# Two model blocks on one core: two gate columns projected with the weights stationary, and a stage's first tile taken in two passes

## The chip, the cores and the metric

The program runs on 1 core of one Trainium2 chip. The metric is the device time of one execution in microseconds (us); lower is better. The time before is the median of 3 runs.

## The reference

The input is one sequence of 256 tokens with 1024 features, in float32. Two chains of layers are computed on it. The first is two layers of (a gated feed-forward block, a mixer, another feed-forward block), each around a residual and RMS norms. The mixer projects the normed tokens with one wide matrix and feeds a gated delta rule (GDN) and a convolution:

```python
p = h @ mix_w_in[i]
qkv, z, beta_logit, a_logit, glu_in, gates = jnp.split(p, SPLITS, axis=-1)
...
qkv = jax.nn.silu(causal_dwconv(qkv, conv_w))
beta = jax.nn.sigmoid(beta_logit.astype(jnp.float32))
g = -jnp.exp(a_log) * jax.nn.softplus(a_logit + dt_bias)
...
y = (g_a * y_a + g_b * y_b) @ mix_w_out[i]
x = x + rmsnorm(y, mix_norm_post[i])
```

`beta_logit` and `a_logit` are 8 columns each: together 16 columns of the 8208 of `mix_w_in`. They are called the gate columns here. The second chain has four layers, each a mixer (`gla`, `mla`, `conv`, `gla`), a squared-ReLU feed-forward block with 4096 hidden features (`mlp`), and a small gated block (`ple`):

```python
x = layer_norm(ALPHA * x + h, ln_g[i, 0], ln_b[i, 0])
x = layer_norm(ALPHA * x + jnp.square(jax.nn.relu(x @ mlp_w1[i])) @ mlp_w2[i], ln_g[i, 1], ln_b[i, 1])
x = x + jax.nn.sigmoid(x @ ple_w_gate[i]) * (p[i] @ ple_w_proj[i])
```

## The kernel before

**Tiles and precision.** The 256 tokens are two tiles of 128 (`NT` = 2, tile 0 and tile 1). The 1024 features are eight chunks of 128 (`KC` = 8). TensorE multiplies float32 as sums of three products: each operand is split into a high part (rounded, `..._hi`) and a low part (the rest, `..._lo`), and the kernel adds high x high, high x low and low x high. `h_hi`/`h_lo` are the two parts of the input of a stage, features on partitions and tokens along the free side.

**Weights.** All weights lie in one list of 128x1024 units. SyncE loads each unit into one of eight slots, ScalarE makes its high part (`weights`, L1459 to L1462) and VectorE its low part (L2007 to L2011); TensorE waits on the semaphore `w_lo` in `next_unit` and frees the slot through `w_used`. In the projections to q, k and v of the mixer only five slots are in use. The engines carry no scheduler: each engine's code is a list of stages (`STAGES`), and the order in which its instructions are written is the order in which they run; engines meet only at semaphores.

**How a stage begins.** The end of a stage leaves x (or its normed copy, or the mixer's y) with tokens on partitions. TensorE transposes a tile in two halves of four chunks (`begin_half` L656, `turn_half` L758), ScalarE copies each half out of PSUM as `h_hi` (L1490, L1493, L1499) and VectorE subtracts it from PSUM to get `h_lo` (L2044, L2048, L2055). TensorE then works on the first tile alone with the first four weight units: it waits for `h_lo` of tile 0, multiplies unit after unit, six matmuls of 512 columns for each, and before the fourth unit it transposes tile 1 (`begin_tile`). Then the same four units run on tile 1, where each unit is freed. This pattern stands in `ffn` (feed-forward stages, 8 of them: `ffn1`, `ffn2` of two layers and `mlp` of four), in `z` (the mixer's first stage, 2), in `project` for the stages whose tag ends in `.out` except the conv layer's (5: mix x2, gla x2, mla) and in `conv` (1). `gla`, `mla`, `gdn_out` and the `.g` branch of `project` have the same pattern in code of their own. In the `.out` stages of gla and mla the transposes of tile 0 come right before, with nothing between. `mlp` begins inside the last units of the product before it.

**The mixer's stages** run in the order z, glu, project16, qkv, mixer. `glu` makes eight chunks of the convolution's input. `project16` makes the gate columns: 48 matmuls, each with a 128x128 piece of `h` stationary and 16 columns of the weight unit moving, out 128 tokens x 16, a bank for each tile. VectorE copies them out (L2272) into `small`; a chain of short operations between VectorE (L2276 to L2285) and ScalarE (L1646 to L1654, with two table loads) follows, whose end (`decays`) is waited for by TensorE in `qkv` at chunk 8. `qkv` makes 24 chunks; for each, ScalarE takes the product out (L1624, L1627), VectorE does three taps of the short convolution (L2241) and a weight unit's low part, and ScalarE a Silu (L1634). Beside that VectorE has the 31 taps of the long convolution (`conv_taps`, L2319): a generator from which each `next` issues two operations. They are spread by hand over `glu`, `qkv` and `mixer`. `mixer` starts on TensorE with two weight units of the gates' products (`side`) and then waits for the last Silu of `qkv`.

## Time and profile before

| | us |
|---|---|
| median of 3 runs (lowest, highest) | 2905.0 (2901.14, 2905.58) |
| the profiled execution, its own time | 2903.36 |
| its span (first to last instruction) | 2901.5 |
| TensorE busy with matmuls | 2822.3 (97%) |
| VectorE busy, ScalarE busy | 1924.0, 1543.1 |

The mean granted clock of TensorE in that execution is 0.991 of full speed. A row of the timeline gives the start and the duration in us, the engine (PE = TensorE matmul, PEld = its weight loads, DVE = VectorE, ACT = ScalarE, POOL = GpSimd), the line of the kernel, the operation with out<-in and shapes, and in brackets the time for which the engine was idle before it, with what released it. Since matmuls overlap, the pace of TensorE is the distance from start to start, not the duration. Moving columns stand last in a matmul's shape: `128*16 128x256` is a stationary operand of 128 rows and 16 columns with 256 columns moving. Names in a matmul's row stand as out<-moving,stationary.

### The profile page before, as it was taken

To read this page: it belongs to the slowest core of one execution; us is meant where nothing else is said; L and a number is where in the kernel's file an instruction comes from. 1 tells how busy PE (TensorE), PEld (TensorE's weight loads), DVE (VectorE), ACT (ScalarE), POOL (GpSimd) and SP (SyncE) were. 2 spreads that over 40 slices of the span, in tenths; PEclk is the share of its full clock that TensorE was granted. 3 is DMA by queue.
4 is the path that set the end of the run, shared out by engine and by line. 5 is a ranking of instruction groups with operands and counts; after the bars stand their busy time and mean duration, and the time that the engine had idled before them with its cause. 6 is when DMAs were issued, how large, how long until landed. Compare 5 with 4: busy or idle time off the path is not lost.

```text
span 2901.5 us, 37886 instructions
## 1 busy us (share of the span) xinstructions
PE 2822.3 (97%) x15012; PEld 2386.3 (82%) x15012; DVE 1924.0 (66%) x2836; ACT 1543.1 (53%) x2389; POOL 71.8 (2%) x99
## 2 busy tenths in 40 slices
PE   8999999999999999999999999999999999999999
PEld 7879988788788799887888878887888888887887
DVE  5556998865565579888655864575546664577545
ACT  6544755565555547555555544454555454564544
POOL 0000000000000000000000000000000000000000
PEclk9999999999999999999999999999999999999999
DMA  8544420465465434115655345552654555542652
GB/s 299 187 139 165 162 73 23 174 208 188 151 218 187 169 122 153 52 42 205 210 188 184 131 157 188 174 187 96 214 188 168 185 198 186 183 161 94 207 184 78
DMA packets 127808, 470.00 MB, mean 162 GB/s; under 512 B 14494, under 2 KB 14654, under 8 KB 126480
## 3 DMA queue, kind: packets, MB, share of 16 engines
q1 hardware_dynamic: 124560, 453.08, 46.0%
q0 software_dynamic: 3072, 14.51, 1.4%
q8 instruction: 119, 1.95, 0.3%
q14 instruction: 57, 0.47, 0.1%
HBM read 466.48 MB, written 1.05 MB: 161 GB/s over the span
## 4 chain that ended last, share of the span: by engine, by line
PE 83%; DVE 11%; ACT 4%; issue 2%; POOL 0%; DMA 0%; POOLq 0%; DVEq 0%; SPq 0%; ACTq 0%
PE ps L619 79%; DVE w_lo_part L2011 2%; PE ps L785 2%; DVE conv_acc L2241 1%; DVE hc L2319 1%; ACT w_hi_part L1462 1%; PE ps L656 1%; DVE wx_lo_part L2011 1%; PE ps L1070 0%; DVE h_lo_part L2044 0%; ACT wx_hi_part L1462 0%; DVE x_res L2153 0%; DVE x_res L2211 0%; DVE x_res L2189 0%; POOL stats L2816 0%
## 5 line engine op out<-in xcount | busy, mean ns | idle before, releaser
L2011 DVE TENSOR_TENSOR w_lo_part<-w_raw,w_hi_part 128x1024 fp32r<-128x1024 f32 x459 | 552.5, 1216 | 317.0 <-ACT w_hi_part L1462 314.2
L1462 ACT ACTIVATE w_hi_part<-w_raw 128x1024 fp32r<-128x1024 f32 x459 | 478.6, 1057 | 355.0 <-PE ps L619 354.7
L619 PE MATMUL ps<-w_hi_part,h_hi_part 128*128 128x512 f32 (+1 forms) x1348 | 538.8, 400 | 24.7 <-DVE h_lo_part L2048 5.4
L619 PE MATMUL ps<-w_hi_part,h_lo_part 128*128 128x512 f32 (+1 forms) x1348 | 525.7, 390 | 0.0
L619 PE MATMUL ps<-w_lo_part,h_hi_part 128*128 128x512 f32 (+1 forms) x1348 | 525.2, 390 | 0.0
L2011 DVE TENSOR_TENSOR wx_lo_part<-wx_raw,wx_hi_part 128x1024 fp32r<-128x1024 f32 x222 | 268.3, 1220 | 193.5 <-ACT wx_hi_part L1462 191.8
L1462 ACT ACTIVATE wx_hi_part<-wx_raw 128x1024 fp32r<-128x1024 f32 x222 | 231.8, 1055 | 227.2 <-PE ps L619 226.9
L619 PEld LDWEIGHTS ps<-w_hi_part,h_hi_part 128*128 128x128 f32 x1348 | 255.9, 190 | 81.9 <-issue 12.5
L619 PEld LDWEIGHTS ps<-w_hi_part,h_lo_part 128*128 128x128 f32 x1348 | 256.1, 190 | 53.9
L619 PEld LDWEIGHTS ps<-w_lo_part,h_hi_part 128*128 128x128 f32 x1348 | 256.5, 190 | 47.8
L619 PE MATMUL ps<-wx_hi_part,h_hi_part 128*128 128x512 f32 x684 | 273.4, 400 | 7.1 <-ACT lv L1804 2.2
L619 PE MATMUL ps<-wx_lo_part,h_hi_part 128*128 128x512 f32 x684 | 268.2, 392 | 0.0
L619 PE MATMUL ps<-wx_hi_part,h_lo_part 128*128 128x512 f32 x684 | 268.2, 392 | 0.0
L619 PE MATMUL ps<-w_hi_part,hid_hi_part 128*128 128x512 f32 x528 | 206.1, 390 | 0.0
L619 PE MATMUL ps<-w_hi_part,hid_lo_part 128*128 128x512 f32 x528 | 205.5, 389 | 0.0
L619 PE MATMUL ps<-w_lo_part,hid_hi_part 128*128 128x512 f32 x528 | 205.4, 389 | 0.0
L2319 DVE SCALAR_TENSOR_TENSOR hc<-glu,cols,hc 128x256 f32<-128x256 f32 x480 | 198.5, 478 | 0.0
L619 PE MATMUL ps<-h_hi_part,w_hi_part 128*128 128x256 f32 (+1 forms) x680 | 195.5, 287 | 0.0
L619 PE MATMUL ps<-h_lo_part,w_hi_part 128*128 128x256 f32 (+1 forms) x680 | 194.5, 286 | 0.0
L619 PE MATMUL ps<-h_hi_part,w_lo_part 128*128 128x256 f32 (+1 forms) x680 | 194.4, 286 | 0.0
L619 PEld LDWEIGHTS ps<-wx_hi_part,h_hi_part 128*128 128x128 f32 x684 | 130.0, 190 | 36.1 <-issue 6.9
L2007 DVE SCALAR_TENSOR_TENSOR w_lo_part<-w_raw,cols,w_hi_part 128x512 fp32r<-128x512 f32 x110 | 82.6, 751 | 106.2 <-ACT w_hi_part L1460 106.2
(437 smaller groups left out, 4860.6 us busy)
## 6 DMA issues: line engine op xcount, KB each, us to landing
w_raw<-in_weights SPq DMA_DIRECT2D x569, 512.0 KB, 3.3
wx_raw<-in_weights SPq DMA_DIRECT2D x288, 512.0 KB, 3.3
row<-in_rows POOLq DMA_DIRECT2D x8, 1024.0 KB, 5.3
row<-in_rows POOLq DMA_DIRECT2D x8, 512.0 KB, 4.0
const<-in_const SPq DMA_DIRECT2D x1, 1088.0 KB, 8.5
x_res<-in_x SPq DMA_DIRECT2D x2, 512.0 KB, 5.3
ple_p<-in_p POOLq DMA_DIRECT2D x4, 256.0 KB, 5.1
out<-x_res SPq DMA_DIRECT2D x2, 512.0 KB, 2.6
```

Of the source, the lines that this page charges most:

```text
L619: return nc.tensor.matmul(out, lhsT, rhs_, start=start, stop=stop, skip_group_check=True)
L656: last_ = nc.tensor.transpose(turned_bank(t, b)[:, c, :], src[:, t, (4 * b + c) * P:(4 * b + c + 1) * P], ident)
L785: last_ = nc.tensor.transpose(hid_bank(c, blk // 2)[:, blk % 2, t * P:(t + 1) * P], hid[:, c % 2, t, blk * P:(blk + 1) * P], ident)
L1462: A(hi_of(s)[:, 0:wd], raw_of(s)[:, 0:wd], ACT.Copy).then_inc(*up("w_hi", u))
L2007: V.scalar_tensor_tensor(lo_of(s)[:, 0:BANK], raw_of(s)[:, 0:BANK], scale[0], hi[:, 0:BANK], ALU.mult, ALU.subtract)
L2011: V.tensor_tensor(lo_of(s)[:, 0:wd], raw_of(s)[:, 0:wd], hi[:, 0:wd], ALU.subtract).then_inc(*up("w_lo", u))
L2241: ins = V.scalar_tensor_tensor(cacc[:, c % 2, :], pre[:, c % 2, k:k + SEQ], col(("convw", i), c * CONV1 + k), cacc[:, c % 2, :], ALU.mult, ...
L2319: ins = V.scalar_tensor_tensor(hc[:, c, :], glu[:, c, k:k + SEQ], w, hc[:, c, :], ALU.mult, ALU.add)
```

## The change

The gate columns are computed turned: 16 weight columns stationary, 256 tokens moving, 24 matmuls into one bank, 16 partitions x 256. ScalarE copies the result to a free corner of `hc`, and after the first chunk of `qkv` TensorE transposes it back in two small transposes (`turn_small`) for VectorE. VectorE's weight unit and three steps of the long convolution, which stood ahead of the copy, now stand in the middle of the gate chain; ScalarE's weight unit stands behind its copy. TensorE's wait for `small` moves from chunk 2 to chunk 3.

The first tile of a stage is taken in two passes over its first four units in `ffn`, `z`, `conv` and the `.out` branch: first the 16 matmuls with `h_hi`, which wait only for `h_hi`; then the 8 with `h_lo`. Tile 1 is transposed after half of the second pass. Tile 1 is computed as before.

```diff
+            def row_high(s, out, hi, tok, start):
+                for n in range(2):
+                    c = slice(n * BANK, (n + 1) * BANK)
+                    mm(out(n), hi[:, tok], hi_of(s)[:, c], start, False)
+                    mm(out(n), hi[:, tok], lo_of(s)[:, c], False, False)
+            def row_low(s, out, lo, tok):
+                for n in range(2):
+                    mm(out(n), lo[:, tok], hi_of(s)[:, n * BANK:(n + 1) * BANK], False, False)
+            def first_tile(slots, out, what, between):
+                tok = slice(0, P)
+                pe.wait_ge(*when("h_hi", what))
+                for k in range(4):
+                    slots.append(next_unit())
+                    row_high(slots[k], out, h_hi[:, k, :], tok, k == 0)
+                pe.wait_ge(*when("h_lo", what))
+                for k in range(4):
+                    if k == 2:
+                        between()
+                    row_low(slots[k], out, h_lo[:, k, :], tok)
...
-                for t in range(NT):
-                    for j in range(4):
-                        if j % 2 == 0:
-                            pe.wait_ge(*when("h_lo", (tag, t, j // 2)))
-                        if t == 0:
-                            slots.append(next_unit())
-                        if t == 0 and j == 3:
-                            begin_tile(tag, 1)
-                        last_ = up_unit(slots[j], 0, j, t)
+                for j in range(4):
+                    if j % 2 == 0:
+                        pe.wait_ge(*when("h_hi", (tag, 0, j // 2)))
+                    slots.append(next_unit())
+                    up_unit(slots[j], 0, j, 0, low=False)
+                for j in range(4):
+                    if j == 2:
+                        begin_tile(tag, 1)
+                    if j % 2 == 0:
+                        pe.wait_ge(*when("h_lo", (tag, 0, j // 2)))
+                    up_unit(slots[j], 0, j, 0, high=False)
...
             def project16(tag):
                 pe.wait_ge(*when("evacuated", (tag + ".z", 1)))
                 s = next_unit()
+                out = ps[0:16, 2, 0:SEQ]
+                for k in range(KC):
+                    c = slice(k * 16, (k + 1) * 16)
+                    mm(out, hi_of(s)[:, c], h_hi[:, k, :], k == 0, False)
+                    mm(out, hi_of(s)[:, c], h_lo[:, k, :], False, False)
+                    last_ = mm(out, lo_of(s)[:, c], h_hi[:, k, :], False, k == KC - 1)
+                last_.then_inc(*up("w_used", ("small", tag)))
+            def turn_small(tag):
+                pe.wait_ge(*when("small_out", tag))
                 for t in range(NT):
-                    for k in range(KC):
...
+                    last_ = nc.tensor.transpose(ps[:, 3, t * 16:(t + 1) * 16], hc[0:16, KC - 1, t * P:(t + 1) * P], ident[0:16, 0:16])
+                last_.then_inc(*up("turned", ("small", tag)))
...
             def project16(tag):
+                act.wait_ge(*when("w_used", ("small", tag)))
+                A(hc[0:16, KC - 1, :], ps[0:16, 2, 0:SEQ], ACT.Copy).then_inc(*up("small_out", tag))
                 weights(1)
```

TensorE at the start of the first gla layer's `.out` stage, before; behind these rows come the other three units, six matmuls each, with the transposes of tile 1 (L758) ahead of the fourth:

```order
L758 MATMUL ps<-const,xn 128x128 [waits y]
L758 MATMUL ps<-const,xn 128x128 x3
L619 MATMUL ps<-w_hi_part,h_hi_part 128x512 [waits w_lo,h_lo]
L619 MATMUL ps<-w_lo_part,h_hi_part 128x512
L619 MATMUL ps<-w_hi_part,h_lo_part 128x512
```

The same place, the change (`turn_half` is L781 there); the first three rows open the pass over four units, and the rows with `h_lo_part` are the second pass around the transposes of tile 1:

```order
L619 MATMUL ps<-w_hi_part,h_hi_part 128x512 [waits w_lo,h_hi]
L619 MATMUL ps<-w_lo_part,h_hi_part 128x512
L619 MATMUL ps<-w_hi_part,h_hi_part 128x512
...
L619 MATMUL ps<-w_hi_part,h_lo_part 128x512 [waits h_lo]
L619 MATMUL ps<-w_hi_part,h_lo_part 128x512 x3
L781 MATMUL ps<-const,xn 128x128 [waits y]
L781 MATMUL ps<-const,xn 128x128 x3
...
L619 MATMUL ps<-w_hi_part,h_lo_part 128x512 x4
```

The first wait is now for `h_hi` alone. The transposes of tile 1 stand after 20 matmuls instead of 18, and 4 matmuls of tile 0 are left behind them instead of 6.

VectorE from the last chunk of `glu` to the start of `qkv` in the first layer, before:

```order
L2011 TENSOR_TENSOR w_lo_part<-w_raw,w_hi_part 128x1024 [waits w_hi] x2
L2319 SCALAR_TENSOR_TENSOR hc<-glu,cols,hc 128x256 [waits conv] x8
L2011 TENSOR_TENSOR w_lo_part<-w_raw,w_hi_part 128x1024 [waits w_hi]
L2272 COPY small<-ps 128x32 [waits w_used]
...
L2281 TENSOR_SCALAR small<-small 128x2x8 [waits a_in]
L2283 TENSOR_TENSOR small<-small 128x2x8 [waits softplus,v_step]
```

The same place, the change (the line numbers of the kernel after):

```order
L2052 TENSOR_TENSOR w_lo_part<-w_raw,w_hi_part 128x1024 [waits w_hi] x2
L2362 SCALAR_TENSOR_TENSOR hc<-glu,cols,hc 128x256 [waits conv] x2
L2312 COPY small<-ps 128x32 [waits turned]
...
L2321 TENSOR_SCALAR small<-small 128x2x8 [waits a_in]
L2052 TENSOR_TENSOR w_lo_part<-w_raw,w_hi_part 128x1024 [waits w_hi,v_step]
L2362 SCALAR_TENSOR_TENSOR hc<-glu,cols,hc 128x256 [waits conv] x6
L2326 TENSOR_TENSOR small<-small 128x2x8 [waits softplus]
```

Six of the eight tap operations and the weight unit's low part moved from ahead of the copy to the place where VectorE waits for ScalarE's softplus; the work is the same.

## Rows read from the trace of the kernel before

**Rows 1.** The page, part 1: TensorE's busy time, share and instructions.
```profile
PE 2822.3 (97%) x15012; PEld 2386.3 (82%) x15012; DVE 1924.0 (66%) x2836; ACT 1543.1 (53%) x2389; POOL 71.8 (2%) x99
```

**Rows 2.** Who TensorE waited for: total us, times, longest (VectorE at L2355, in `gdn_out`).
```profile
PE ps L619 <- DVE gdn_w L2355: 7.0, 2, 3.5
```

**Rows 3.** Stretches: length; busy (instructions) of PE, PEld, DVE, ACT, POOL; clock; DMA.
```profile
279.30:285.20 5.90, 5.90 (x50) 5.90 (x48) 4.76 (x9) 2.36 (x3) 0.00 (x0) 0.88 0.33 103
285.30:290.50 5.20, 5.20 (x25) 5.20 (x26) 3.24 (x9) 3.51 (x7) 0.00 (x0) 0.50 0.53 179
1579.90:1582.70 2.80, 2.80 (x25) 2.23 (x24) 2.80 (x3) 1.06 (x1) 0.00 (x0) 1.00 0.93 315
```

**Rows 4.** Timeline of VectorE from the end of `glu` into `qkv`.
```profile
283.20 3.25 DVE L2319 SCALAR_TENSOR_TENSOR hc<-glu,cols,hc 128x256 f32<-128x256 f32 x8
286.61 1.22 DVE L2011 TENSOR_TENSOR w_lo_part<-w_raw,w_hi_part 128x1024 fp32r<-128x1024 f32 x1 [0.16 <-ACT w_hi_part L1462]
287.75 0.18 DVE L2272 COPY small<-ps 128x32 f32<-128x32 f32 x1
...
291.69 0.17 DVE L2283 TENSOR_TENSOR small<-small 128x16 f32<-128x16 f32 x1 [2.85 <-ACT small L1654]
...
292.33 1.53 DVE L2241 SCALAR_TENSOR_TENSOR conv_acc<-conv_pre,cols,conv_acc 128x256 f32<-128x256 f32 x3 [0.25 <-ACT conv_acc L1627]
...
319.23 1.53 DVE L2241 SCALAR_TENSOR_TENSOR conv_acc<-conv_pre,cols,conv_acc 128x256 f32<-128x256 f32 x3 [0.47 <-ACT conv_acc L1627]
...
362.72 1.52 DVE L2241 SCALAR_TENSOR_TENSOR conv_acc<-conv_pre,cols,conv_acc 128x256 f32<-128x256 f32 x3
```

**Rows 5.** Timeline of TensorE where `mixer` begins.
```profile
363.81 0.39 PE L619 MATMUL ps<-w_hi_part,h_lo_part 128*128 128x512 f32 x1
364.75 1.16 PE L619 MATMUL ps<-const,gdn_gate 128*128 128x128 f32 x8 [0.55 <-ACT qkvT L1634]
```

**Rows 6.** Stretches behind three idle times of TensorE, columns as in rows 3.
```profile
1319.50:1324.70 5.20, 5.20 (x16) 4.51 (x17) 5.20 (x6) 1.37 (x2) 0.57 (x1) 0.50 0.63 187
1679.80:1683.10 3.30, 3.30 (x9) 2.55 (x8) 1.07 (x3) 0.00 (x0) 0.00 (x0) 0.50 0.00 0
...
2657.50:2661.00 3.50, 3.49 (x15) 2.91 (x16) 2.15 (x5) 0.00 (x0) 0.46 (x1) 1.00 0.02 5
```

**Rows 7.** Timeline, first tile of the first gla layer's `.out` stage: ScalarE, VectorE, TensorE.
```profile
1676.32 0.60 ACT L1499 ACTIVATE h_hi_part<-ps 128x512 fp32r<-128x512 f32 x1 [2.52 <-PE ps L758]
...
1677.99 1.28 DVE L2055 TENSOR_TENSOR h_lo_part<-ps,h_hi_part 128x512 fp32r<-128x512 f32 x2
...
1678.73 0.50 PE L619 MATMUL ps<-w_hi_part,h_hi_part 128*128 128x512 f32 x1 [1.67 <-DVE h_lo_part L2055]
```

**Rows 8.** The same stage, tile 1: transposes, `h_lo`, its first matmul.
```profile
1684.55 1.03 PE L758 MATMUL ps<-const,xn 128*128 128x128 f32 x8
...
1685.82 1.29 DVE L2055 TENSOR_TENSOR h_lo_part<-ps,h_hi_part 128x512 fp32r<-128x512 f32 x2 [4.94 <-ACT h_hi_part L1499]
...
1686.80 0.39 PE L619 MATMUL ps<-w_hi_part,h_hi_part 128*128 128x512 f32 x1
```

**Rows 9.** Timeline, start of `z` in the first layer: ScalarE and TensorE.
```profile
204.80 2.17 ACT L1493 ACTIVATE h_hi_part<-ps,cols 128x128 fp32r<-128x128 f32 x8 [1.74 <-PE ps L656]
...
207.33 0.79 PE L619 MATMUL ps<-w_hi_part,h_hi_part 128*128 128x512 f32 x1 [2.13 <-DVE h_lo_part L2048]
```

**Rows 10.** Timeline of TensorE, first matmul of mla's `.out` stage.
```profile
1992.50 0.50 PE L619 MATMUL ps<-w_hi_part,h_hi_part 128*128 128x512 f32 x1 [0.97 <-DVE h_lo_part L2055]
```

**Rows 11.** Timeline, first `mlp` stage: TensorE's third unit, VectorE's x, tile 1's first matmul.
```profile
1707.59 0.50 PE L619 MATMUL ps<-wx_hi_part,h_hi_part 128*128 128x512 f32 x1 [0.23 <-DVE h_lo_part L2044]
...
1708.27 1.41 DVE L2211 SCALAR_TENSOR_TENSOR x_res<-xn,stats,row 128x512 f32<-128x512 f32 x2 [0.67 <-POOL stats L2816]
...
1711.62 0.39 PE L619 MATMUL ps<-w_hi_part,h_hi_part 128*128 128x512 f32 x1
```

**Rows 12.** Timeline, `ffn2` of the first layer: tile 1's first matmul.
```profile
608.52 0.50 PE L619 MATMUL ps<-w_hi_part,h_hi_part 128*128 128x512 f32 x1 [1.57 <-DVE h_lo_part L2044]
```

More of the change, by code:

```diff
@@ L731, in project, with turn_second @@
                         turn_half(ready, 0, 1)
[L732 to L742 removed]
+                    def turn_second():
+                        turn_half(ready, 1, 0)
+                        turn_half(ready, 1, 1)
+                    first_tile(slots, lambda n: out(0, n), (ready, 0, 0), turn_second)
+                    pe.wait_ge(*when("h_lo", (ready, 1, 0)))
+                    for k in range(4):
+                        row_chunk(slots[k], out, h_hi[:, k, :], h_lo[:, k, :], 0, k == 0, False, tiles=[1]).then_inc(*up("w_used"))
                     for t in range(NT):
@@ L894, in z @@
                 slots = []
-                for t in range(NT):
-                    pe.wait_ge(*when("h_lo", (tag, t, 0)))
-                    for k in range(4):
-                        if t == 0:
-                            slots.append(next_unit())
-                        if t == 0 and k == 3:
-                            begin_tile(tag, 1)
-                        last_ = row_chunk(slots[k], out, h_hi[:, k, :], h_lo[:, k, :], 0, k == 0, False, tiles=[t])
-                        if t == 1:
-                            last_.then_inc(*up("w_used"))
+                first_tile(slots, lambda n: out(0, n), (tag, 0, 0), lambda: begin_tile(tag, 1))
+                pe.wait_ge(*when("h_lo", (tag, 1, 0)))
+                for k in range(4):
+                    row_chunk(slots[k], out, h_hi[:, k, :], h_lo[:, k, :], 0, k == 0, False, tiles=[1]).then_inc(*up("w_used"))
                 for t in range(NT):
@@ L1355, in conv, with up_unit @@
             def conv(tag, j):
-                def up_unit(s, c, j, t):
+                def up_unit(s, c, j, t, high=True, low=True):
                     tok = slice(t * P, (t + 1) * P)
@@ L2269, in project16 @@
             def project16(tag):
-                weights(1)
-                dve.wait_ge(*when("w_used", ("small", tag)))
-                V.tensor_copy(small[:, 0:2, :], ps[:, 2:4, 0:16]).then_inc(*up("small", tag))
+                dve.wait_ge(*when("turned", ("small", tag)))
+                V.tensor_copy(small[:, 0:2, :], ps[:, 3, 0:32].rearrange("p (t n) -> p t n", t=NT)).then_inc(*up("small", tag))
                 dve.wait_ge(*when("small", tag))
@@ L2281, in project16 @@
                 link(V.tensor_scalar(small[:, 12:14, 0:GH], small[:, 2:4, 0:GH], 0.0, None, ALU.max))
+                weights(1)
+                for _ in range(3):
+                    next(taps[0])
                 dve.wait_ge(*when("softplus", tag))
@@ L2297, in glu_ @@
                     if c >= 4:
-                        for _ in range(4):
+                        for _ in range(4 if c < KC - 1 else 1):
                             next(taps[0])
```

77 lines of the change are left out of this document (37 added, 40 removed).

## The prediction

> **What bounds the kernel now.** I read the page first: TensorE is busy 97% of the span [rows 1], so only two things can be saved: work of TensorE itself, and the short waits between stages. The list of who TensorE waited for shows that these are single waits of 0.2 to 3.5 us [rows 2, 7]. Then I read the places the change touches in the timeline. The reader should look at starts, since TensorE's pace is start to start.
>
> **Gate columns, on TensorE.** The 48 narrow matmuls fill 279.3 to 285.3, 6.0 us [rows 3]. They go at the pace of their weight loads, not of their 16 columns: the stretch has 48 loads in 5.9 us. And they bring the clock down: it is 0.88 of full in that stretch and 0.50 (1.2 GHz) in the 5.2 us behind it, where 25 matmuls of `qkv` take 5.2 us. The turned form exists already in gla: its 24 matmuls take 2.8 us at clock 1.00 [rows 3]. At full clock the 25 matmuls of `qkv` would take 25 x 0.12 = 3.0 us (0.12 is 2.8/24 rounded up). So TensorE saves 6.0 - 2.8 = 3.2 us and 2.2 us of slow clock, and pays some 0.2 us for two small transposes: 5.2 us in each of the two mixers.
>
> Here a rule speaks against the change. The rows show 48 matmuls of 16 columns at 0.12 us each [rows 3]. The Trainium skill (TensorE: Matmul & The Clock Gate, "Wait — 56ns, not 53.3ns?") says that back-to-back matmuls start as little as about 25 ns apart when they are narrow; by that floor alone 48 would be an estimated 1.2 us, and turning them into 24 of 256 columns would lose time. The measured pace is five times that floor, so the rows decide. None of the sum rests on this page.
>
> **Gate columns, on the path.** What TensorE saves isn't what the kernel saves. The mixer's first matmul waits for the last Silu of `qkv`, and is already 0.55 us late [rows 5]: VectorE works through `qkv` almost without a pause from 292.33 to 362.72, 23 chunks in 70.4 us, 3.06 us each, where TensorE needs 24 x 0.12 = 2.9 us [rows 4]. So `mixer` starts when VectorE is done, and the question is how much earlier VectorE starts `qkv`. Before: eight tap operations 283.20 to 286.45, the weight unit to 287.8, copy at 287.75, short chain, 2.85 us idle for softplus, then `qkv` at 292.33. After: two tap operations end at about 284.0. The copy waits for TensorE: turned products 279.3 to 282.1, first chunk of `qkv` 2.9 us to 285.0, transposes and their latency 0.4 us, copy at 285.4. The short operations take 1.1 us (287.75 to 288.84, where the idle time of 2.85 us begins), to 286.5; the weight unit 1.1, to 287.6; six tap operations 6 x 0.41 = 2.45 (3.25/8), to 290.05. Softplus comes 3.8 us after the copy's end (287.93 to 291.69; ScalarE has two table loads in it), so at 285.6 + 3.8 = 289.4, and is hidden. `qkv` then starts 0.6 us behind, as before (291.69 to 292.33): 290.6, 1.7 us earlier. The pause of 0.47 us at 319.23 [rows 4] came from TensorE's late chunk and goes. So each mixer starts 2.2 us earlier, not 5.2. The three other us become idle time of TensorE ahead of `mixer`: 0.55 + 5.2 - 2.2 = about 3.5 us.
>
> **A price that the trace of before doesn't show at this place.** TensorE's idle times of 3.5 us elsewhere [rows 2] have the clock at 0.50 behind them for 5.2 us of work (the first of [rows 6]). Below, nothing is lost if the clock holds, as it did behind an idle time of 1.7 us in the second gla layer (1.00) while it fell behind the same one in the first (0.50) [rows 6]. Above, 5.2 us at half speed lose 2.6 us, if all of it is on the path. The start of `mixer` is mostly TensorE bursts, with ScalarE and VectorE beside them; I take 2.0 us, nearer the upper end, since the idle time is like the 3.5 us one. The gate part is then worth 2 x (2.2 - 2.0) = 0.4 us, of which both ends are 2 x 2.2 = 4.4 and 2 x (-0.4) = -0.8.
>
> **Waiting for `h_hi` only.** Gain by stage, from the first matmul's new start:
> - gla `.out`, twice: `h_hi` ends at 1676.92, so the first matmul can start at about 1677.0; it now starts at 1678.73, because VectorE begins `h_lo` only at 1677.99 [rows 7]. Gain 1.7 us each. The second pass needs `h_lo` after 16 matmuls, 3.6 us, when it is long there. In the first of them the clock fell to 0.50 for 3.3 us [rows 6]; with 1.7 us less idle I expect it to hold, another 1.65 us (half of 3.3), once.
> - mla `.out`: idle 0.97 us [rows 10], of which `h_lo`'s first half, about 0.7 us, goes.
> - `z`, twice: eight copies in 2.17 us from 204.80, so half 0 is there at 205.9, against 207.33 now [rows 9]. But 1.3 us earlier at slow clock is three matmuls, 0.7 us at full clock, and the next point takes 0.45 of it: 0.3 us each.
> - `mlp`, four times: before, the third unit waits for `h_lo` of half 1 (a gap of 0.23 us, and as much for restarting) [rows 11]; the first pass fills it. Gain 0.45 us each, about as much as tile 1 can take: VectorE gives its x from 1708.27 on, so TensorE's transposes can't move, and tile 1's first matmul comes at 1711.15 instead of 1711.62.
> - `ffn2` twice and `ffn1` of layer 1: tile 1 is 1.57 us late for VectorE's reasons [rows 12]: nothing.
> - `mix` `.out` twice, `conv`, first stage: no wait for `h_lo` there, or one for weights: nothing.
>
> **What the new order costs.** Tile 1's transposes come after 20 matmuls instead of 18, with 4 behind them instead of 6. Before: transposes at 1684.55, `h_lo` of half 0 at 1686.47, first matmul at 1686.80, 0.33 us later [rows 8]. Now two matmuls of cover, 0.45 us, are gone: TensorE waits 0.15 to 0.2 us. That takes 0.2 from each of the gla and mla gains and makes the four stages without a gain 0.2 us longer each. It is inside the figures given for `z` and `mlp`.
>
> Sum of the first tiles: 2 x 1.5 + 0.5 + 2 x 0.3 + 4 x 0.45 - 4 x 0.2 = 5.1, and 1.65 of clock: 6.75 us. With the gates' 0.4: 7.15 us. Against the profiled execution's own 2903.36 us (1.6 below the median of 2905.0) that is **2896.2 us**, said as 2896.
>
> **The rivals.**
> 1. The clock holds at the mixer's start, and comes back sooner at `z`. For it: stretches behind similar idle times fell and held [rows 6]. Against: the longest idle times fell. Gain 4.4 + 6.75 + up to 2 x 1.7 (half of 3.4) = 11 to 14.5, say 2891. The 1.7 is half of a stretch like the 3.3 us one [rows 6].
> 2. TensorE's saving goes through whole, because VectorE has slack in `qkv` that I don't see: 2 x 5.2 + 6.75 = 17, 2886. Against: VectorE's pace of 3.06 us a chunk [rows 4] and the wait at 364.75 [rows 5].
> 3. Tile 1 eats the gains: VectorE's and ScalarE's order is unchanged, so an earlier TensorE waits for the next thing of theirs (y, x, `h_lo` of tile 1), and no clock is won. Half of 5.1 and -0.8 for the gates, 2901.5. For it: `ffn2`'s wait of 1.57 us [rows 12]. Against: in gla, TensorE reaches tile 1's transposes at 1677.0 + 20 x 0.23 = 1681.6, and y of tile 1 is VectorE's next work behind the `h_lo` that ends at 1679.27 [rows 7], 2.3 us before.
> 4. Slower: the first pass asks for four weight units in 2.7 us (12 matmuls) instead of 4.1 us (18). If a stage's third and fourth units were split only behind the stage's start, each would cost ScalarE and VectorE 1.1 to 1.2 us, some 2.3 us in 15 stages: 34 us, 2930. It decides if VectorE has a weight unit between the last product and the first tile's units. Against: the first gla tile ran 18 matmuls behind its start with no wait for `w_lo`, and VectorE has none between rows 7 and rows 8.
>
> **How the numbers follow.** My forecast gets 0.55, rival 1 0.20, rival 2 0.04, rival 3 0.19, rival 4 0.02. The range takes the forecast with its bounds (4.4 to -0.8 for the gates, clock won or not), rival 1 to 2889 and rival 3 to 2902; outside are rivals 2, 4 and some of the scatter of 4 us that the runs before have among themselves: **2889 to 2902**. A measurement of this kernel tells about 0.2% from no change, 5.8 us: faster means under 2899.2. That is most of the forecast (0.50 of 0.55), rivals 1 and 2 and nothing of rival 3: 0.74. Same 0.24, slower 0.02.
>
> **What the profile after would show.** Right: 24 matmuls of shape 128*16 128x256 in 2.8 us at clock 1.00 and no 0.50 stretch behind them; VectorE without the 2.85 us idle, with one of about 1.4 us ahead of its copy; TensorE idle about 3.5 us at the start of `mixer`, probably with 0.50 behind it; the first matmul of gla `.out` 0.1 us behind `h_hi`; 0.1 to 0.3 us waits at tile 1. Wrong: a mixer start that moves by 5 us, waits of TensorE on `w_lo` in first tiles, or a clock that falls at the turned form after all.

## The result, and the profile after

The kernel before took 2905.0 us (median of 5 runs, 2901.14 to 2905.58), the changed one 2889.43 (2885.91 to 2890.74): ratio 0.9949, with a 95% interval of 0.9938 to 0.996. The profiled execution of the changed kernel took 2885.91 us with a span of 2884.0, which is 17.5 less than the span before. Its mean granted clock is 0.996; before it was 0.991. So the time fell by 15.6 us where 9 were forecast: the sign is right, the time lies at the low end of the range, and most of this text is on where the other 7 us come from.

The page, part 1:

```profile
PE 2808.7 (97%) x14968; PEld 2371.0 (82%) x14968; DVE 1923.6 (67%) x2836; ACT 1542.2 (53%) x2391; POOL 71.9 (2%) x99
```

TensorE's busy time fell by 13.6 us [rows 1], with only 44 matmuls fewer. Two pieces of that are the gate columns. Stretches of the changed kernel (columns as in rows 3): the turned products, the work behind them, and the start of the mixer.

```profile
278.40:281.20 2.80, 2.80 (x27) 2.33 (x27) 1.56 (x2) 2.37 (x3) 0.00 (x0) 1.00 0.00 0
281.30:286.50 5.20, 5.20 (x44) 5.04 (x43) 3.81 (x10) 3.08 (x6) 0.00 (x0) 1.00 0.62 202
360.10:365.30 5.20, 5.20 (x39) 4.94 (x40) 4.85 (x14) 4.43 (x19) 0.82 (x1) 1.00 0.69 249
```

The products take 2.8 us instead of 6.0, and the clock is 1.00 behind them where it was 0.50: 44 matmuls in 5.2 us instead of 25 [rows 3]. That much was forecast. The third row was not: the clock holds at the mixer's start too.

VectorE around the gate columns, and its first chunk of `qkv`; the last row is its last chunk:

```profile
282.40 0.87 DVE L2362 SCALAR_TENSOR_TENSOR hc<-glu,cols,hc 128x256 f32<-128x256 f32 x2
284.49 0.19 DVE L2312 COPY small<-ps 128x32 f32<-128x32 f32 x1 [1.22 <-PE ps L953]
...
285.62 1.22 DVE L2052 TENSOR_TENSOR w_lo_part<-w_raw,w_hi_part 128x1024 fp32r<-128x1024 f32 x1
286.76 2.46 DVE L2362 SCALAR_TENSOR_TENSOR hc<-glu,cols,hc 128x256 f32<-128x256 f32 x6
289.14 0.17 DVE L2326 TENSOR_TENSOR small<-small 128x16 f32<-128x16 f32 x1
...
289.57 1.52 DVE L2282 SCALAR_TENSOR_TENSOR conv_acc<-conv_pre,cols,conv_acc 128x256 f32<-128x256 f32 x3
```

The idle time of 2.85 us ahead of softplus [rows 4] is gone, and one of 1.22 stands ahead of the copy: both as forecast. But between 289.57 and the mixer's start VectorE has no idle time over 0.2 us any more. Before there were two, of 0.47 us at 319.23 [rows 4] and of 1.41 us at 327.01, and the forecast counted only the first. The second one, before:

```profile
327.01 1.53 DVE L2241 SCALAR_TENSOR_TENSOR conv_acc<-conv_pre,cols,conv_acc 128x256 f32<-128x256 f32 x3 [1.41 <-ACT conv_acc L1627]
```

TensorE at the mixer's start, after:

```profile
357.74 0.39 PE L619 MATMUL ps<-w_hi_part,h_lo_part 128*128 128x512 f32 x1
360.10 1.16 PE L619 MATMUL ps<-const,gdn_gate 128*128 128x128 f32 x8 [1.97 <-ACT qkvT L1673]
```

It waits 1.97 us there, not 3.5, and the mixer starts 4.65 us earlier than before [rows 5]. Tile 1 of `z` already starts 0.80 us earlier than before (215.94 against 216.74), so 3.85 belong to the gates' part, where the forecast had 2.2.

The first tiles. The three lines are the start of `z`, of the first gla `.out` stage and of mla's `.out`:

```profile
206.86 0.80 PE L619 MATMUL ps<-w_hi_part,h_hi_part 128*128 128x512 f32 x1 [0.80 <-ACT h_hi_part L1532]
...
1667.14 0.50 PE L619 MATMUL ps<-w_hi_part,h_hi_part 128*128 128x512 f32 x1
...
1977.10 0.50 PE L619 MATMUL ps<-w_hi_part,h_hi_part 128*128 128x512 f32 x1 [0.25 <-ACT h_hi_part L1538]
```

`h_lo` no longer holds any of the three. `z` waits 0.80 us for ScalarE's `h_hi` instead of 2.13 for `h_lo` [rows 9], mla 0.25 instead of 0.97 [rows 10], and gla's matmul starts without idle time, where it had waited 1.67 [rows 7]; it stands 0.05 us behind the end of `h_hi`:

```profile
1666.49 0.60 ACT L1538 ACTIVATE h_hi_part<-ps 128x512 fp32r<-128x512 f32 x1 [2.51 <-PE ps L781]
```

In the gla stage the first matmul stands 1.34 us behind the first transpose (1665.80) instead of 3.11 (1675.62): 1.77 us, forecast 1.7. The price, tile 1 of gla and of `z`:

```profile
1671.83 1.03 PE L781 MATMUL ps<-const,xn 128*128 128x128 f32 x8
1672.62 1.17 PE L619 MATMUL ps<-wx_hi_part,h_lo_part 128*128 128x512 f32 x4
1673.84 0.50 PE L619 MATMUL ps<-w_hi_part,h_hi_part 128*128 128x512 f32 x1
```

```profile
215.94 0.50 PE L619 MATMUL ps<-w_hi_part,h_hi_part 128*128 128x512 f32 x1 [1.04 <-DVE h_lo_part L2089]
```

In gla the four matmuls behind the transposes need 0.92 us at full pace and the next one comes 1.22 after them: 0.3 us of waiting, forecast 0.15 to 0.2. In `z` the distance from start to start is 1.43 us, where it was 0.97: 0.46, the whole of the two matmuls of cover.

**The clock.** A list of all stretches at 0.50 in the two profiles shows what else changed. Before, behind the start of the program and ahead of its last matmul: 6.83 us long at 205.3, 283.8, 983.5, 1062.0, 1318.0 and 2304.5, 3.41 at 543.2, 1679.8 and 1939.2. After: 3.41 at 206.5, 537.5 and 977.9, 6.83 at 1309.0 and 2288.6. Half of TensorE's busy time in them is 22.4 us before and 10.6 us after. So up to 11.8 of the 17.5 us are clock. Two of the stretches (283.8 and 1062.0) went with the narrow matmuls; whether the others went for a reason or by chance one profile can't say.

### The profile page after: what moved, and what is told of

Its sections match the earlier page's. It is cut to its first block, busy times and chain, and to the rows that moved or that the text cites. A ratio compares the mean times of both kernels' runs of the same rounds, so it can differ in the third digit from the quotient of the medians.

```text
span 2884.0 us, 37784 instructions
## 1 busy us (share of the span) xinstructions
PE 2808.7 (97%) x14968; PEld 2371.0 (82%) x14968; DVE 1923.6 (67%) x2836; ACT 1542.2 (53%) x2391; POOL 71.9 (2%) x99
## 4 chain that ended last, share of the span: by engine, by line
PE 81%; DVE 13%; ACT 4%; issue 2%; POOL 0%; DMA 0%; POOLq 0%; SPq 0%; DVEq 0%; ACTq 0%
PE ps L619 77%; DVE w_lo_part L2052 3%; DVE conv_acc L2282 2%; PE ps L810 2%; DVE hc L2362 2%; PE ps L681 1%; ACT w_hi_part L1501 1%; DVE wx_lo_part L2052 1%; PE ps L1102 0%; ACT wx_hi_part L1501 0%; DVE h_lo_part L2085 0%; DVE x_res L2252 0%; POOL stats L2859 0%; DVE gdn_w L2398 0%; DVE x_res L2194 0%
## 5 line engine op out<-in xcount | busy, mean ns | idle before, releaser
L619 PE MATMUL ps<-w_hi_part,h_hi_part 128*128 128x512 f32 x1316 | 530.6, 403 | 20.0 <-DVE h_lo_part L2085 4.6
L619 PE MATMUL ps<-w_lo_part,h_hi_part 128*128 128x512 f32 x1316 | 516.2, 392 | 0.0
L619 PE MATMUL ps<-w_hi_part,h_lo_part 128*128 128x512 f32 x1316 | 505.2, 392 | 0.0
L619 PEld LDWEIGHTS ps<-w_hi_part,h_hi_part 128*128 128x128 f32 x1316 | 249.5, 190 | 79.8 <-issue 12.9
L619 PEld LDWEIGHTS ps<-w_hi_part,h_lo_part 128*128 128x128 f32 x1316 | 246.7, 188 | 52.3
L619 PEld LDWEIGHTS ps<-w_lo_part,h_hi_part 128*128 128x128 f32 x1316 | 249.9, 190 | 47.7
```

Source lines behind the costliest of these rows:

```text
L619: return nc.tensor.matmul(out, lhsT, rhs_, start=start, stop=stop, skip_group_check=True)
```

## The experiments

### The two parts, and the two halves of the gates' part

Four kernels, on one chip, each with 11 runs beside 33 of the kernel before (median 2903.24). `e1_gates` is the kernel before with every edit on the gate columns; `e2_passes` with every edit on first tiles; `e3_form` has the turned product, but VectorE's order as before:

```diff
             def project16(tag):
                 weights(1)
-                dve.wait_ge(*when("w_used", ("small", tag)))
-                V.tensor_copy(small[:, 0:2, :], ps[:, 2:4, 0:16]).then_inc(*up("small", tag))
+                dve.wait_ge(*when("turned", ("small", tag)))
+                V.tensor_copy(small[:, 0:2, :], ps[:, 3, 0:32].rearrange("p (t n) -> p t n", t=NT)).then_inc(*up("small", tag))
```

(TensorE's and ScalarE's side of the form is as in the change), and `e4_order` keeps the 48 narrow matmuls, with VectorE's new order around its old copy; the three steps of the long convolution are taken from the last chunk of `glu`:

```diff
             def project16(tag):
-                weights(1)
                 dve.wait_ge(*when("w_used", ("small", tag)))
...
+                weights(1)
+                for _ in range(3):
+                    next(taps[0])
                 dve.wait_ge(*when("softplus", tag))
```

**e1_gates.** 

> The gate columns' part alone (turned products, moved VectorE work, transposes back); first tiles as before. Theory A (VectorE's chain through qkv sets the mixer's start, and its start of qkv and its two pauses moved): each mixer starts 3.85 us earlier than before against the stage z (start of mixer minus start of tile 1 in z: 144.2 us instead of 148.0), TensorE idle about 2 us there, clock not at 0.50 behind it; 2 x 3.85 = 7.7 us, time near 2897. Theory B (the two parts only work together, the gates' part alone gives what the prediction said, 0.4 us): mixer 2.2 us earlier and a slow stretch behind it, 2904. Theory C (TensorE's 5.2 us per mixer go through): 2894.

**e2_passes.** 

> The two passes of first tiles alone; gate columns as before. Theory A (parts are additive; the trace of the whole change puts 17.5 us of span against before, 7.7 of them at the gates and 1.5 at a slow stretch that wanders): 8 us, 2897, of which z gives 1.7 to 2.3 us each, the gla .out stages 1.8 to 2.9 each, mla .out 0.4, mlp 0.3 to 0.5 each, and the first stage, conv and mix .out lose 0.2 to 1 us each. Rival (z's gain comes from the gates' part or is a matter of chance in the clock; the prediction's 0.3 each stands): z 0.3 each, sum 5 us, 2900.

**e3_form.** 

> The turned form alone: 24 matmuls with 256 columns, transposed back, but VectorE's weight unit and eight tap operations ahead of its copy as before. Theory A (VectorE sets the mixer's start): VectorE starts qkv at about the same time as before (292.3), so only the pauses of 0.47 and 1.41 us inside qkv can go: mixer 0.5 to 1.9 us earlier each, 1 to 4 us in all, 2901 to 2904; TensorE idle 3.9 to 5.2 us ahead of the mixer, and by the prediction's reading of the clock a 0.50 stretch behind it, which takes up to 2 us back. Theory C (TensorE's saving counts): mixer 5 us earlier, 2894.5.

**e4_order.** 

> VectorE's moved order alone: weight unit and six tap operations inside the gate chain; 48 narrow matmuls as before. Theory A: VectorE starts qkv 1.7 to 2 us earlier than 292.3, but TensorE is late by its own work (the 6.0 us and the slow clock remain), so the mixer can start only 0.55 us earlier, the idle time there: 0 to 1 us in all, 2904 to 2905. If TensorE lags, VectorE's pause in qkv grows instead. Rival (the order alone brings the 3.85 us): 2897.

Measured: e1_gates 2897.51 us (ratio 0.998, 0.9971 to 0.9989), e2_passes 2899.61 (0.9987, 0.9978 to 0.9996), e3_form 2900.25 (0.999, 0.9981 to 0.9998), e4_order 2901.42 (0.9997, 0.9988 to 1.0006, so no gain is shown for it).

In e1_gates the mixer starts 144.17 us behind tile 1 of `z`, where it was 148.01 before, and 3.84 earlier in the second layer too. That is theory A (3.85), and not B (2.2) or C (5.2). By the medians the kernel is 5.7 us faster than the one before, where theory A had 7.7; the clock, below, is where A was wrong. The halves show how it is made up. VectorE's two pauses inside `qkv` in e4_order, where the narrow matmuls stayed:

```profile
319.76 1.53 DVE L2241 SCALAR_TENSOR_TENSOR conv_acc<-conv_pre,cols,conv_acc 128x256 f32<-128x256 f32 x3 [0.99 <-ACT conv_acc L1627]
...
327.54 1.52 DVE L2241 SCALAR_TENSOR_TENSOR conv_acc<-conv_pre,cols,conv_acc 128x256 f32<-128x256 f32 x3 [1.42 <-ACT conv_acc L1627]
```

and in e3_form, with the turned product but the old order:

```profile
293.24 0.17 DVE L2293 TENSOR_TENSOR small<-small 128x16 f32<-128x16 f32 x1 [2.85 <-ACT small L1664]
...
323.92 1.52 DVE L2251 SCALAR_TENSOR_TENSOR conv_acc<-conv_pre,cols,conv_acc 128x256 f32<-128x256 f32 x3
...
326.71 1.52 DVE L2251 SCALAR_TENSOR_TENSOR conv_acc<-conv_pre,cols,conv_acc 128x256 f32<-128x256 f32 x3
```

So the form alone removes both pauses (0.47 + 1.41 = 1.88 us) and leaves the 2.85 us idle; the order alone removes the 2.85 and leaves, even lengthens, the pauses. Behind tile 1 of `z` the mixer of e4_order starts 1.5 us earlier than before in the first layer, where the slow stretch behind the narrow matmuls was 3.41 us long, and 0.1 later in the second, where it was 6.83: TensorE's lateness takes back what VectorE's order wins. Together they give the 3.85: VectorE begins `qkv` at 289.57 instead of 292.33, 1.96 us earlier beside the 0.80 from before, and 1.88 are the pauses. Why the second pause goes, ScalarE shows. Before, from chunk 9 (counted from 0) to the Silu ahead of chunk 11:

```profile
318.45 0.39 ACT L1624 ACTIVATE conv_pre<-ps 128x256 f32<-128x256 f32 x1 [2.66 <-PE ps L619]
...
323.05 1.28 ACT L1631 ACT_TABLE_LOAD   x1
324.34 0.27 ACT L1631 ACTIVATE gdn_gate<-gdn_gate 128x80 f32<-128x80 f32 x1
324.63 1.28 ACT L1634 ACT_TABLE_LOAD   x1
325.92 0.42 ACT L1634 ACTIVATE qkvT<-conv_acc 128x256 f32<-128x256 f32 x1
```

and the changed kernel:

```profile
316.98 1.28 ACT L1670 ACT_TABLE_LOAD   x1
319.71 0.27 ACT L1670 ACTIVATE gdn_gate<-gdn_gate 128x80 f32<-128x80 f32 x1 [1.46 <-DVE gdn_gate L2295]
320.00 1.28 ACT L1673 ACT_TABLE_LOAD   x1
```

The Exp of the decays needs a table of its own, one load ahead of it and one behind. Before, ScalarE had waited 2.66 us for TensorE's late chunk, so it came to the Exp late, and both loads (2.9 us with the Exp) stood ahead of the next chunk for VectorE. Now TensorE is ahead, ScalarE is through with its chunk sooner, and the first load runs while ScalarE would wait for VectorE anyway (the 1.46 us ahead of the Exp). In e3_form the Exp waits in the same way, for 1.54 us, and in e4_order both loads stand ahead of the next chunk as before: the pause goes with the form. That the table loads are its middle link is read from these rows; no run removed them alone. (The Trainium skill, ScalarE: Activation LUTs, "What ACT_TABLE_LOAD costs", gives 1283 ns for the load and 1380 ns of draining, 2.66 us for a switch. The trace agrees with the 1.28; the drain isn't seen, since the Exp begins 1.29 us behind the load's start.)

e3_form speaks against C as well: TensorE's whole saving is there, but the mixer starts only 2.1 us earlier (against tile 1 of `z`), and the other 3.2 are wait, 4.11 us from start to start instead of 0.94:

```profile
364.44 1.86 PE L619 MATMUL ps<-const,gdn_gate 128*128 128x128 f32 x7 [3.72 <-ACT qkvT L1642]
```

The clock is another matter. In e1_gates it fell at the mixer's start in both layers, behind the same wait of 2.37 us at which it had held in the changed kernel. The first layer's stretch:

```profile
362.90:368.10 5.20, 5.20 (x33) 5.20 (x33) 4.38 (x13) 3.98 (x18) 0.36 (x1) 0.67 0.65 240
```

And the slow stretch at 1679.8, which the prediction wanted to remove by a shorter idle time, is in none of e1_gates, e3_form and e4_order, though their gla `.out` stage waits for `h_lo` as before. So it was a matter of the one profile, not of the idle time alone. In e2_passes the first matmul of `z` comes 1.88 us behind the first transpose instead of 3.23, yet little of that is left at the mixer: `z` to `mixer` takes 160.21 and 160.42 us instead of 160.65 and 160.79, and both `z` have their 6.83 us slow as before. The prediction's 0.3 for `z` is met there, and e2_passes' own theory A (1.7 to 2.3) is not; its median, 3.6 us under the kernel before, is nearer the 5 of its rival than the 8 of A. The gla and mla stages gain in it what they gain in the whole change: the first matmul of gla `.out` comes 1.34 us behind the first transpose in both gla layers.

### Is it chance? The changed kernel again, and z undone

`e5_again` and `e11_third` are the changed kernel unedited, with the next kernels on their chips; `e8_zold` is the changed kernel with the old first tile in `z` alone; `e6_t18` transposes tile 1 two matmuls sooner:

```diff
                 for k in range(4):
-                    if k == 2:
+                    if k == 1:
                         between()
                     row_low(slots[k], out, h_lo[:, k, :], tok)
...
-                    if j == 2:
+                    if j == 1:
                         begin_tile(tag, 1)
```

and `e7_taps` moves three steps of the long convolution:

```diff
-                    if c % 2:
+                    if c % 2 and c > 3:
                         next(taps[0])
...
-                        for _ in range(4 if c < KC - 1 else 1):
+                        for _ in range((4, 4, 6, 2)[c - 4]):
                             next(taps[0])
```

**e5_again.** 

> The changed kernel itself once more, unedited. The two parts alone gave 5.7 and 3.6 us by their medians, 9.4 together, where the whole change gave 15.6 in another comparison; its records had a mean clock of 0.994 to 0.996, those of the parts 0.990 to 0.994. Theory D (the parts work together: only in the whole change does the clock hold at the mixer's start and come back sooner in z): median near 2888, clock 0.994 or more in nearly all runs, slow stretches behind the mixer's start in none. Rival E (which idle time is followed by slow clock is largely chance, and the profiled run was a lucky one): median 2890 to 2894, clocks from 0.991 to 0.996, and the profile shows a slow stretch at places where the first had none.

**e6_t18.** 

> The changed kernel with the transposes of tile 1 after 18 matmuls again (the first half of the second pass is two matmuls, six stand behind the transposes), in all four places. Theory (the wait at tile 1 is the two matmuls of cover): in z the wait from start to start falls from 1.43 to 0.97 us, the waits at tile 1 of mla's and gla's .out go, each of the 15 stages gains 0 to 0.46 us where VectorE's x is not what it waits for: 1.5 to 4 us in all against the changed kernel, 2886. Rival (x or y of tile 1 comes too late for an earlier transpose, the wait only moves ahead of the transposes): same as the changed kernel within 1 us.

**e7_taps.** 

> The changed kernel with three steps of the long convolution (two operations each, 0.81 us a step) moved by hand into VectorE's idle times in glu (2.10 us ahead of chunk 7, 1.22 ahead of the copy): two of them out of the first chunks of qkv, one out of the end of the mixer. Theory A (VectorE sets the mixer's start): mixer starts 2 x 0.81 = 1.6 us earlier, the wait there falls from 2.36 to 0.8 us from start to start, and the wait for the last tap before the mixer's end shrinks by up to 0.8: 2 x (1.6 + 0.8) = 4.8 us at most, 2885. Rival (something else, ScalarE's Silus or TensorE, sets the start): less than 1 us each.

**e8_zold.** 

> The changed kernel with z's first tile in the old order. By the profiles of the whole change z gave 1.67 and 2.29 us. Theory (the whole of it is z's earlier start of 1.3 us at the first matmul plus a slow stretch of 3.41 instead of 6.83 us, less 0.46 at tile 1): this kernel is 3 to 4 us slower than the changed one, and has 6.83 us slow in both z. Rival (what the clock gave was chance; the shift of the first matmul is nearly given back): 0.6 to 1.7 us slower.

Measured, 5 runs each beside a kernel before of 2902.86 us: e5_again 2890.55 (0.9956, 0.9942 to 0.9969), e6_t18 2888.52 (0.9952, 0.994 to 0.9965), e7_taps 2885.27 (0.9942, 0.9929 to 0.9954), e8_zold 2892.99 (0.9966, 0.9954 to 0.9979).

The change is there again with its two repeats (0.9949, 0.9956, 0.9947 with e11_third below). e5_again goes to rival E. Its profile has slow clock where the first had none, at the second layer's mixer (stretch of e5_again):

```profile
1135.74:1140.94 5.20, 5.20 (x32) 5.20 (x33) 3.64 (x9) 3.20 (x18) 0.00 (x0) 0.67 0.69 212
207.50:214.20 6.70, 6.00 (x14) 4.75 (x15) 3.83 (x12) 2.71 (x9) 2.37 (x4) 0.50 0.25 79
```

and its first `z` is slow for 6.83 us, the second row, while e11_third, the same program, has the same place like this:

```profile
207.50:214.20 6.70, 6.33 (x23) 5.11 (x24) 3.50 (x11) 2.38 (x8) 2.37 (x4) 0.75 0.29 83
```

23 matmuls against 14 in the same 6.7 us. So the place of the slow clock is in part chance, but not chance alone. From the first transpose of `z` to the mixer's start, in us, with the slow time in `z`:

| | layer 1 | layer 2 |
|---|---|---|
| before | 160.65 (6.83) | 160.79 (6.83) |
| e2_passes | 160.21 (6.83) | 160.42 (6.83) |
| e1_gates | 156.51 (6.83) | 156.71 (6.83) |
| e8_zold | 156.48 (6.83) | 156.48 (6.83) |
| changed kernel | 155.13 (3.41) | 154.65 (3.41) |
| e5_again | 156.56 (6.83) | 155.29 (3.41) |
| e11_third | 155.14 (3.41) | 154.70 (3.41) |

With the old first tile, `z` had 6.83 us slow in all 10 cases of five kernels (the one before, e1_gates, e3_form, e4_order, e8_zold, two layers each). With the new one it had 3.41 in 9 of 16 (eight profiles). Where it stays 6.83 the new order gives 0 to 0.4 us, and where it is 3.41 it gives 1.2 to 2.0. So the earlier start doesn't only pull matmuls into slow time: with it full clock often comes back sooner. The profiles show that the two go together, not why. e8_zold's median is 2.4 us above e5_again's, between its theory (3 to 4) and its rival (0.6 to 1.7), with overlapping intervals.

At the mixer's start with a wait of about 2.4 us the clock fell in 6 of 12 cases (e1_gates 2, e8_zold 2, e5_again 1, e6_t18 1; the changed kernel and e11_third none), and the mixer's first part grew by 0.5 us in e1_gates' first layer, by 1.2 in e5_again's second. The six are not spread evenly: with the old first tile in `z` (e1_gates, e8_zold) it fell in 4 of 4, with the new one in 2 of 8. The order of first tiles in `z` may thus bear on the clock at the mixer as well, 155 us later; 12 cases can't settle it.

e6_t18: the wait at tile 1 of `z` is 0.97 from start to start again, as expected:

```profile
214.61 0.50 PE L619 MATMUL ps<-w_hi_part,h_hi_part 128*128 128x512 f32 x1 [0.57 <-DVE h_lo_part L2089]
```

Its median is 2.0 us better than e5_again's, at the low end of what was expected, and the intervals overlap. Of that 1.55 us are seen in the traces: 0.46 in each `z`, and 0.21 in each of gla (twice) and mla, where the wait at tile 1 is gone (gla from the first transpose to tile 1's first matmul 7.83 us instead of 8.04). The rest is not told apart from the clock.

e7_taps confirms theory A where its work went as planned. First layer:

```profile
358.47 0.39 PE L619 MATMUL ps<-w_hi_part,h_lo_part 128*128 128x512 f32 x1
359.39 1.16 PE L619 MATMUL ps<-const,gdn_gate 128*128 128x128 f32 x8 [0.53 <-ACT qkvT L1673]
```

The wait fell from 2.36 to 0.92 from start to start, and that for the last tap of the convolution from 1.98 to 1.17. In the second layer the wait only fell to 1.94: there `glu`'s idle times of VectorE are 2.20 and 2.11 us ahead of chunks 5 and 6 and none ahead of 7, so steps put behind chunk 6 only made it later. The kernel is 5.3 us better than e5_again by the medians, where at most 4.8 were expected; 3.5 of them are seen in the traces (1.45 and 0.41 at the two mixers, 0.8 at the last tap of each), and the rest is not told apart from the clock.

### The price of the clock at 3.6 us of idle time, and the best version

`e10_idle` brings about the idle time that the prediction had expected at the mixer:

```diff
-                    if c % 2:
+                    for _ in range(2 if c in (5, 7) else c % 2):
                         next(taps[0])
```

`e9_best` is e6_t18 with e7_taps' edit, its numbers by layer:

```diff
-                        for _ in range(4 if c < KC - 1 else 1):
+                        for _ in range(((4, 4, 6, 2), (5, 5, 4, 2))[i][c - 4]):
```

**e10_idle.** 

> The changed kernel with two more steps of the long convolution (2 x 0.81 us of VectorE) in the middle of qkv, taken from its end in the mixer: TensorE's wait ahead of the mixer becomes 2.36 + 1.63 = 4.0 us from start to start, 3.6 idle, which is the idle time of the prediction. The prediction's price: slow clock behind it in both layers, 2.0 us each. Theory now (five slow stretches of 3.41 us behind waits of 2.4 us cost 0.5 to 1.2 us each from the mixer's start to its last tap, 1.3 and 1.8 behind waits of 4.1 us): slow in both layers, 1.3 to 1.8 us each. Apart from the clock, the mixer starts 1.63 later and the last tap is 1.63 earlier in VectorE's chain, so most of that comes back at the wait for the last tap (1.98 before): sum 3 to 5 us slower than the changed kernel by either, or 1 to 2 if the clock costs nothing there.

**e9_best.** 

> Both improvements together: the transposes of tile 1 after 18 matmuls, and three steps of the long convolution earlier, this time by a table for each layer (4, 4, 6, 2 steps behind chunks 4 to 7 of glu in the first layer, 5, 5, 4, 2 in the second, since there VectorE's idle time lies ahead of chunks 5 and 6). Theory A: as the two alone (2.0 and 5.3 us against the changed kernel by their medians), 6 to 7.5 us, and the second layer's mixer wait falls from 2.37 to about 0.9 us as the first one's did (it was 1.94 with one table for both): 2882 to 2885. Rival (the two share their gain, since a stage can only be as early as VectorE): 2885 or more.

**e11_third.** 

> The changed kernel once more, unedited, as the measure for the two beside it and for a third profile of its clock: by theory E (chance) 2888 to 2892, with slow stretches behind z's start of 3.41 us in about half the cases and 6.83 in the others, and behind the mixer's start in about half.

Measured, 5 runs each, the kernel before 2904.78 us beside them: e10_idle 2891.14 (0.9956, 0.9943 to 0.9968), e9_best 2884.5 (0.9935, 0.9921 to 0.9949), e11_third 2887.96 (0.9947, 0.9934 to 0.9959).

TensorE at the first mixer of e10_idle, and the stretches behind the start in both layers:

```profile
363.97 1.44 PE L619 MATMUL ps<-const,gdn_gate 128*128 128x128 f32 x5 [3.61 <-ACT qkvT L1673]
```

```profile
363.97:369.20 5.23, 5.23 (x24) 5.23 (x25) 3.60 (x8) 3.14 (x18) 0.00 (x0) 0.50 0.70 245
1139.00:1144.20 5.20, 5.20 (x24) 5.20 (x25) 3.59 (x8) 3.11 (x18) 0.00 (x0) 0.50 0.66 236
```

24 matmuls in 5.2 us, where the changed kernel had 39 [its row above]. The next matmul that waits for VectorE (operand `gdn_w`) comes 29.60 us behind the mixer's start instead of 27.88: the slow clock costs 1.72 us, and 1.64 in the second layer. The two rows are of e10_idle and of the changed kernel:

```profile
393.57 0.68 PE L619 MATMUL ps<-gdn_w 128*128 128x128 f32 x4 [0.37 <-DVE gdn_w L2479]
```

```profile
387.98 0.79 PE L619 MATMUL ps<-gdn_w 128*128 128x128 f32 x5 [0.60 <-DVE gdn_w L2479]
```

e3_form, with a wait of 4.11 us, has 29.66 there, and 29.19 in the second layer, where the slow stretch was 3.41 us long instead of 6.83. The prediction's price of 2.0 us at 3.5 us of idle time was about right; the idle time was not. The kernel is 3.2 us slower than e11_third, as expected.

e9_best has the short wait in both layers. The second one's:

```profile
1129.36 0.39 PE L619 MATMUL ps<-w_hi_part,h_lo_part 128*128 128x512 f32 x1
1130.31 1.16 PE L619 MATMUL ps<-const,gdn_gate 128*128 128x128 f32 x8 [0.56 <-ACT qkvT L1673]
```

It takes 154.68 and 154.70 us from `z` to the mixer with 6.83 us slow in both, 1.9 less than e5_again's 156.56 in the same case. It is the fastest kernel tried by its median, 20.3 us under the kernel before and 3.5 under e11_third; its interval and e11_third's overlap, so that it beats the changed kernel is likely, not shown by the times alone. Its time lies in the range of its theory A (2882 to 2885) and its second layer's wait fell as expected, but against the changed kernel beside it the gain is 3.5 us, where theory A added up 6 to 7.5: the two gains had been taken against e5_again, where the changed kernel had gained least of its three comparisons. Against e7_taps (2885.27, on another chip) it can't be ranked.

## Why the prediction was right or wrong

**What bounds the kernel.** Right: TensorE stays busy 97%, and everything won is waits between stages, work of TensorE and clock.

**Gate columns on TensorE.** Right in each number: 2.8 us at clock 1.00, the slow stretch behind it gone in both layers and in every kernel with the form, gone in none without it (before, e2_passes, e4_order).

**Gate columns on the path.** The method was right: VectorE sets the mixer's start, not TensorE's 5.2 us. The term was mis-sized at one sentence: "The pause of 0.47 us at 319.23 came from TensorE's late chunk and goes. So each mixer starts 2.2 us earlier". The rows of VectorE through `qkv` hold one more pause, 1.41 us at 327.01, ended by ScalarE; it isn't in the text. It came from TensorE's lateness in the second degree, by way of the table loads, and goes too (e3_form against e4_order). With VectorE's start 1.96 earlier instead of 1.7, the term is 3.85 instead of 2.2.

**The clock's price at the mixer.** The price of 2.0 was near the 1.72 measured by e10_idle, but was put on 3.5 us of idle time. (Of the two idle times of 3.5 us that it was modelled on, one had slow clock for 6.83 us behind it, at 1318.0, the other for 3.41, at 543.2; the text shows only the first.) With 1.65 us more of VectorE's chain gone, 1.97 are left, and behind that the clock falls in half of the cases for 0.5 to 1.2 us. So the gates' term is 2 x 3.85 less some 2 x 0.4, about 7, not 0.4. By medians e1_gates is 5.7 us under the kernel before. The two together, the pause that wasn't counted and the price put on an idle time that shrank with it, carry most of the miss.

**`h_hi` only.** gla `.out` with tile 1: 1675.62 to 1686.80 before, 1665.80 to 1673.84 after, 3.14 us less, of which 1.65 are the slow stretch; 1.49 remain, forecast 1.5. The second gla layer, at full clock in both profiles, has 9.59 (2654.40 to 2663.99) and 8.05 (2638.60 to 2646.65): 1.54. `mlp`: from tile 0's transposes to tile 1's first matmul 9.48 before (1702.14 to 1711.62), 9.01 after (1689.31 to 1698.32): 0.47, forecast 0.45. mla with its `mlp` 0.74, forecast 0.95; conv with its `mlp` 0.4 (2180.39 to 2495.17 before, 2164.97 to 2479.34 after), forecast 0.25: 0.4 are lost at `conv`'s own first tile and 0.8 won behind it. That can't be told from the scatter: e2_passes has -0.1 there, and e11_third, with the slow stretch of `conv` 3.41 us long instead of 6.83, 1.1. `ffn2` and tile 1's transposes there: nothing won, and `mix` `.out` longer by 0.2, as forecast. `z`: 0.3 was the value for slow clock of 6.83 us; it missed that the earlier start halves it in 9 of 16 cases, so that the mean is nearer 1. The 1.65 us of clock at gla stand in the profile before and in none of the three other profiles with the old order there, so the reason given (a shorter idle time lets the clock hold) is not what made them go.

**Order of tile 1.** Right: 0.3 us in gla, 0.46 in `z`, undone by e6_t18.

**The rivals.** The first (the clock holds, comes back sooner at `z`; 2891) came nearest to the time, and its two events happen, each about half of the time; but of the missing 7 us only about half are the clock's price at the mixer; as much is VectorE's earlier end (2 x 1.65), which it doesn't have. The second was right that there was slack in `qkv` which the text didn't see, and wrong on its size: e3_form shows TensorE's saving stopped by VectorE. Of the third only the waits at tile 1 are seen, 0.3 to 0.46 us. The fourth did not occur at its size of 34 us. In the profile after, no first tile waits for `w_lo`, except the program's first matmul, as before; but in three of the other profiles with the new order (e5_again, e10_idle, e11_third) the program's very first tile has one more such wait, 0.3 to 0.5 us, which no profile with the old order has. e11_third's:

```profile
14.74 0.77 PE L619 MATMUL ps<-w_hi_part,h_hi_part 128*128 128x512 f32 x1 [0.45 <-DVE w_lo_part L2049]
```

It is the sign that the prediction named, at one stage of 15.

**The sum.** From the 7.15 us of the prediction to the 17.5 of the two spans: gates 7.3 more (7.7, no clock lost in this profile, instead of 0.4), `z` 3.4 more (1.67 and 2.29 by tile 1, instead of 0.6), a slow stretch at 1939.2 that the profile after doesn't have 1.5, less 0.9 by which the first `z` began later (204.97 instead of 204.10; at the program's start the matmuls go at half pace, 0.43 us each, until 15.3 us instead of 14.1) and 0.7 for the slow stretch of the second layer's `gdn_out`, which held more work (6.83 us of it busy instead of 5.34): 17.8. The last three, 1.65 at gla and a part of `z` are the scatter of one execution; in medians the change is worth 12 to 17 us (12.3, 15.6 and 16.8 in three comparisons), the parts alone 5.7 and 3.6.

**What stays open.** That the parts alone give 9.3 where the whole gives 12 to 17: their clocks (0.990 to 0.994 against 0.993 to 0.996) may hold the difference, but no run shows why they should be lower. One trace of a cause is the count above: with the old first tile in `z`, `z` was slow for 6.83 us in 10 of 10 cases and the mixer's start behind a wait of 2.4 us in 4 of 4, so the gates' part alone pays at both places more often than the whole does. And: what decides in which execution the clock falls behind a wait of 2.4 us; the profiles show it at the same place in one run of a program and not in the next.

## What to carry to other kernels

When an engine's saving is cut off by another engine's chain, read that chain's every idle time, with what ended it, and ask of each whether the saving reaches it by way of a third engine: here 1.4 of 3.85 us did, through ScalarE's table loads. Work that fills a wait is worth placing by the idle times of each layer, since the same table of numbers that gained 1.4 us in one layer gained 0.4 in the other. Before a slow stretch of one profile goes into a sum, look whether its like is slow too (the second gla stage was not); if not, it may be scatter, and more profiles of the same kernel decide.

## What was not expected of the hardware

The same program shows slow clock behind a wait of 2.4 us in one execution and none in another, and comes back from it after 3.41 or after 6.83 us; three profiles of the changed kernel differ by 4.5 us in span (2884.0, 2888.5, 2885.9), with half of TensorE's busy time at slow clock at 10.6, 15.1 and 11.4 us. With the longer wait at the mixer, 4.0 and 4.1 us from start to start, the clock fell in all four cases (e10_idle, e3_form), behind 2.4 in 6 of 12, and behind e7_taps' 1.94 and the waits of 0.94 it held.
